# Attention scores with the head dimension's high and low parts stacked in one 128-row matmul, and all head-1 copies on DVE

## The reference

```
z = jnp.einsum("bqhd,bkhd->bhqk", qb, kb).astype(jnp.float32) * scale
strict = s_pos < t_pos
log_keep = jnp.where(strict, jax.nn.log_sigmoid(-z), 0.0)
after = lax.cumsum(log_keep, axis=3, reverse=True) - log_keep
weights = jnp.where(strict, jnp.exp(jax.nn.log_sigmoid(z) + after), 0.0)
outs.append(jnp.einsum("bhqk,bkhd->bqhd", weights.astype(v.dtype), vb))
```

## Time and profile before

| | us |
|---|---|
| median of 3 runs | 2955.57 (2955.53 to 2959.38) |
| the profiled execution | 2955.53 |
| its span, first to last instruction | 2953.8 |
| PE busy in the span | 2770.1 (94%) |
| DVE busy | 1511.2 (51%) |
| ACT busy | 1077.0 (36%) |
| POOL busy | 985.1 (33%) |
| attention stage, within the span | about 1573 to 2525 |

### The profile page before, as it was taken

The page is one execution under the profiler, slowest core; times in us unless marked ns, Lnnn a source line. Parts: engine busy times, 40 slices in busy tenths (PEclk is TensorE's granted clock), DMA queues, the critical chain, the costliest instruction groups (busy, mean ns, idle before and its releaser), DMA issues. The chain is left out here.

```text
span 2953.8 us, 40091 instructions
## 1 busy us (share of the span) xinstructions
PE 2770.1 (94%) x14914; PEld 2031.1 (69%) x14914; DVE 1511.2 (51%) x1689; ACT 1077.0 (36%) x1590; POOL 985.1 (33%) x694
## 2 busy tenths in 40 slices
PE   4999999999999989979997999999999999689998
PEld 3999999888888857756664555555555555368887
DVE  6112445210000010008996888888889888565554
ACT  4010101111111131101114778777778777432221
POOL 1211121121211200007775655656566556200000
PEclk6999999999999999989997999999999999889999
DMA  3232221323212211114444122121221210342331
GB/s 117 85 116 99 79 71 64 114 107 118 74 64 71 78 58 67 45 45 120 129 128 140 58 58 73 37 87 51 58 87 35 82 30 26 117 137 87 98 99 43
DMA packets 165312, 239.96 MB, mean 81 GB/s; under 512 B 11152, under 2 KB 117904, under 8 KB 157504
## 3 DMA queue, kind: packets, MB, share of 16 engines
q1 hardware_dynamic: 163456, 238.25, 25.2%
q10 hardware_dynamic: 1728, 0.03, 0.0%
HBM read 141.49 MB, written 96.76 MB: 81 GB/s over the span
## 5 line engine op out<-in xcount | busy, mean ns | idle before, releaser
L1399 POOL TENSOR_TENSOR a_w<-a_beta,a_rest 128x1024 f32<-128x1024 f32 (+2 forms) x320 | 560.3, 1751 | 341.3 <-DVE a_rest L1351 311.8
L352 PE MATMUL f_acc<-ut_hi,f_w_hi 128*128 128x512 f32 (+2 forms) x1568 | 582.4, 371 | 14.6 <-POOL f_w_lo L337 14.6
L352 PE MATMUL f_acc<-ut_lo,f_w_hi 128*128 128x512 f32 (+2 forms) x1568 | 584.6, 373 | 0.0
L352 PE MATMUL f_acc<-ut_hi,f_w_lo 128*128 128x512 f32 (+2 forms) x1568 | 583.2, 372 | 0.0
L1351 DVE TENSOR_TENSOR_SCAN a_rest<-a_keep,a_rest,a_ones 128x513 f32<-128x513 f32 x384 | 466.8, 1262 | 11.0 <-ACT a_keep L1321 11.0
L1270 PE MATMUL a_turn<-a_ident,a_w 128*128 128x128 f32 (+1 forms) x2432 | 352.7, 280 | 28.1 <-DVE a_wt L1304 26.0
L1270 PEld LDWEIGHTS a_turn<-a_ident,a_w 128*128 128x128 f32 (+1 forms) x2432 | 257.4, 140 | 123.1 <-issue 64.9
L334 POOL TENSOR_TENSOR f_w_hi<-f_stage,f_zero 128x1024 fp32r<-128x1024 f32 x44 | 83.3, 1893 | 770.7 <-DMA f_stage<-in_w_blocks 770.7
L1285 PE MATMUL a_o<-a_wt,a_v 128*64 128x512 f32 (+3 forms) x1408 | 338.5, 559 | 0.0
L352 PEld LDWEIGHTS f_acc<-ut_hi,f_w_hi 128*128 128x128 f32 x1568 | 295.1, 188 | 51.0 <-issue 15.3
L352 PEld LDWEIGHTS f_acc<-ut_lo,f_w_hi 128*128 128x128 f32 x1568 | 295.0, 188 | 34.7
(11 more groups left out here) (172 smaller groups left out, 3415.8 us busy)
## 6 DMA issues: line engine op xcount, KB each, us to landing
f_stage<-in_w_blocks SPq DMA_DIRECT2D x44, 512.0 KB, 5.5
scratch_gate<-f_row_a SPq DMA_DIRECT2D x16, 1024.0 KB, 4.6
o_g<-scratch_mixed SPq DMA_DIRECT2D x32, 512.0 KB, 5.4
scratch_xbc<-f_row_a SPq DMA_DIRECT2D x12, 1032.0 KB, 4.8
s_xc<-scratch_xbc SPq DMA_DIRECT2D x16, 768.0 KB, 5.3
scratch_k_hi<-f_row_a SPq DMA_DIRECT2D x8, 1032.0 KB, 3.9
scratch_k_lo<-f_row_b SPq DMA_DIRECT2D x8, 1032.0 KB, 6.9
n_xin<-in_x SPq DMA_DIRECT2D x16, 512.0 KB, 3.5
```

The source lines that it names most:

```text
L352: last = nc.tensor.matmul(acc[c][:, 0:tn], w[s][:, k, :], u[:, k, t0:t0 + tn], start=(k == 0 and u is ut_hi and w is w_hi), stop=(k == KB ...
L1399: nc.gpsimd.tensor_tensor(w[r % AS][:, :, 0:tn], beta[r % KEEPS][:, :, 0:tn], rest[r % RS][:, :, 1:tn + 1], ALU.mult).then_inc(w_ready, 1)
```

## The change

Three things are edited, all in the attention stage.

The scores are formed in 128-row matmuls, one head at a time. q_high and q_low of a head lie one over the other, in partitions 0 to 63 and 64 to 127 of a new tile `q`, the two heads beside each other. k_high and k_low are each held twice, in the upper and the lower 64 partitions, again with the heads beside each other. One matmul with k_high gives q_high k_high + q_low k_high, one with k_low gives q_high k_low + q_low k_low, a product that was left out before. That is four matmuls a unit in place of six; in diagonal units a head's mask product follows its two.

The transfers follow the layout: each part of each key tensor is loaded by two transfers of 64 partitions, each reading the whole of what one transfer read before. The queries are read once, as before.

`on_act` is now head 0 alone, so that the second head's copy of every fourth block (11 in a head pair) goes from ACT to DVE.

```diff
--- before.py
+++ after.py
@@ -1115,7 +1115,7 @@
     PADS = [pads(n) for n in range(N + 1)]
 
     def on_act(m, h):
-        return h == 0 or m % 4 == 0
+        return h == 0
 
     EVACS = {engine: [sum((on_act(x // 2, x % 2)) == (engine == "act") for x in range(y)) for y in range(2 * N + 1)]
              for engine in ("act", "dve")}
@@ -1131,9 +1131,9 @@
         def ring(name, n, shape, dt=F32):
             return [m_.sbuf(f"a_{name}{r}", list(shape), dt) for r in range(n)]
 
-        k_high, k_low = ring("k_high", 2, (P, T), F32R), ring("k_low", 2, (P, T), F32R)
+        k_high, k_low = ring("k_high", 2, (P, 2, T), F32R), ring("k_low", 2, (P, 2, T), F32R)
         v = ring("v", 2, (P, NT + 1, P))
-        q_high, q_low = ring("q_high", 2, (P, W), F32R), ring("q_low", 2, (P, W), F32R)
+        q = ring("q", 2, (P, 2, W), F32R)
         gate, out = ring("gate", 2, (P, W)), ring("out", 2, (P, W))
         keep, beta = ring("keep", KEEPS, (P, 2, SIDE)), ring("beta", KEEPS, (P, 2, SIDE))
         rest = ring("rest", RS, (P, 2, SIDE + 1))
@@ -1173,8 +1173,10 @@
                 slot = pair % 2
                 t0, t1 = ((0, W + META), (W + META, T))[part]
                 for tile, name in ((k_high, "k_hi"), (k_low, "k_lo")):
-                    sp.dma_start(tile[slot][:, t0:t1].bitcast(F32),
-                                 scratch[name][pair, :, t0:t1]).then_inc(k_loaded[slot][part], 16)
+                    for half in range(2):
+                        sp.dma_start(tile[slot][half * HEAD:(half + 1) * HEAD, :, t0:t1].bitcast(F32),
+                                     scratch[name][pair, :, t0:t1].rearrange("(h p) t -> p h t", h=2)
+                                     ).then_inc(k_loaded[slot][part], 16)
 
             def load_values(pair):
                 slot = pair % 2
@@ -1185,9 +1187,10 @@
 
             def load_queries(ch):
                 pair, c, r = ch // NW, ch % NW, ch % 2
-                for tile, name in ((q_high, "q_hi"), (q_low, "q_lo")):
-                    sp.dma_start(tile[r][:, :].bitcast(F32),
-                                 scratch[name][pair, :, c * W:(c + 1) * W]).then_inc(q_loaded[r], 16)
+                for half, name in enumerate(("q_hi", "q_lo")):
+                    sp.dma_start(q[r][half * HEAD:(half + 1) * HEAD, :, :].bitcast(F32),
+                                 scratch[name][pair, :, c * W:(c + 1) * W]
+                                 .rearrange("(h p) t -> p h t", h=2)).then_inc(q_loaded[r], 16)
 
             def load_gate(ch):
                 pair, c, r = ch // NW, ch % NW, ch % 2
@@ -1231,20 +1234,17 @@
                 if n == 0 or chunk_of(n - 1) != ch:
                     pe.wait_ge(q_loaded[ch % 2], START + 32 * (ch // 2 + 1))
                     if c < 2:
-                        pe.wait_ge(k_loaded[slot][c], START + 32 * (pair // 2 + 1))
+                        pe.wait_ge(k_loaded[slot][c], START + 64 * (pair // 2 + 1))
                 if n >= 2:
                     pe.wait_ge(beta_ready, START + n - 1)
                 t0 = W * (k + 1) if qi is None else W * k
                 tn = width(n)
-                products = ((q_high, k_high), (q_low, k_high), (q_high, k_low))
-                for i, (q_part, k_part) in enumerate(products):
-                    for h in range(2):
-                        rows = slice(h * HEAD, (h + 1) * HEAD)
-                        mm = nc.tensor.matmul(z[n % 2][:, h, 0:tn], q_part[ch % 2][rows, qb * P:(qb + 1) * P],
-                                              k_part[slot][rows, t0:t0 + tn], start=(i == 0),
-                                              stop=(i == len(products) - 1), skip_group_check=True)
-                if diagonal(n):
-                    for h in range(2):
+                for h in range(2):
+                    for k_part in (k_high, k_low):
+                        mm = nc.tensor.matmul(z[n % 2][:, h, 0:tn], q[ch % 2][:, h, qb * P:(qb + 1) * P],
+                                              k_part[slot][:, h, t0:t0 + tn], start=(k_part is k_high),
+                                              stop=(k_part is k_low), skip_group_check=True)
+                    if diagonal(n):
                         if qi is None:
                             z_part, never_part = z[n % 2][:, h, 0:META], never[:, P - META:P]
                         else:
```

## The result

| kernel | median us | runs | span of the profiled execution |
|---|---|---|---|
| before | 2957.08 (2955.53 to 2959.38) | 4 | 2953.8 |
| after | 3011.78 (3010.36 to 3014.28) | 4 | 3009.1 |

The change makes the kernel slower: ratio 1.0185, 95% interval 1.0168 to 1.0203. That is +54.7 us where +17.5 was forecast, and above the range. The two profiled spans differ by 55.3.

The account below looks back on a forecast made before the run. It took DVE to bound three stretches of each head pair and PE the rest. Copies +1.70 and PE -0.23 gave +1.47 per pair, x 8 = +11.8; key loads +5.8; 2955.5 + 11.8 + 5.8 = 2973.1 us, range 2957 to 2990.

Parts of the forecast that it names:

- The copies, +1.70 per pair: On DVE in attention: 11 head-1 copies a pair moved from ACT cost +1.70 us per pair, bounds 0 and +3.4.
- the three runs: Stretches of a head pair, in chunks 1, 2 and 3, where DVE never stops; copies add +0.17, +0.59 and +0.94.
- The switch regained: On PE: changing from 64 to 128 rows costs about 0.10 ahead of the turns and 0.05 in them, regained by the edit.
- The rival in which neither comes back: On PE: neither switch nor short passes regained, about +2.2 us per pair more, +18 us, 2991; chance 0.10.
- 4 x 0.228 + 0.054 for one load: PE's new scores in a full off-diagonal unit: four passes and one weight load, 0.97 us where it was 0.91.
- the units that I had named as PE's: Units where PE sets the pace: second of chunk 0 to last diagonal of chunk 1, last three diagonals of chunks 2, 3.
- -0.23: PE's whole term per head pair, from the diagonal units where PE sets the pace: a gain of 0.23 us.
- My upper bound, +0.5 to +1.1: PE's term per pair if a narrow 128-row pass can't go under the 0.11 us of a pair of loads.
- Off the diagonal +0.01 to +0.03: PE's extra time in each full off-diagonal unit, in us; +0.17 if the switch were not regained, mostly hidden either way.
- Ahead of it stand 2.11 MB more: +5.8: Start of attention: doubled key loads delay chunk 1's first unit by 5.8 us at 364 GB/s.
- My bound of +10: Upper bound in us on the keys' loads at the start, if 64-partition transfers are slower and the clock rises later.
- Later pairs ... free, for the queue's next transfers too: Key loads of later pairs cost nothing: issued a pair (120 us) ahead, with DMA busy a fifth of the stage.

Follow-up runs that it names:

- the run with the masks last: The changed kernel with both mask products behind both heads' scores in diagonal units, as the kernel before has them: 3005.91 us, ratio 1.0165.
- keys' transfers halved: The kernel before with every key transfer split into two of 64 partitions, bytes and layout unchanged: 2961.27 us, ratio 1.0014.

## Why the prediction was wrong

- **Direction and place: right.** Slower, in the pairs and at the start, nowhere else.
- **The copies, +1.70 per pair: right.** Alone they cost +1.67. The count from start to start, the three runs and the gaps held, run by run (0.19, 0.59 and 0.93 for 0.17, 0.59 and 0.94), so this isn't luck; DVE's waits for ACT above 0.5 are gone.
- **The switch regained: right.** From the last pass to the turns 0.24, the turns 0.96 (forecast 0.97 behind full-height work). The rival in which neither comes back is refuted by the first of these.
- **"4 x 0.228 + 0.054 for one load": wrong, the first failed step.** I halved the 0.108 of two loads. They had run side by side, so one load shows the same 0.11. The Trainium skill, "TensorEngine Tiling (Array Packing)", Key Properties, has the rule that I passed over, in the same short list as the one that I cited: different tiles can load weights and multiply in parallel. The load rows agree (0.19 for two half-height loads, 0.19 for one full one). In the changed kernel a unit's first pass is 0.34, and no narrow pass falls below 0.11. From scores to turns the diagonal units take, as medians over the stage, before and after: 144 columns 0.61 and 0.66, 272: 0.70 and 0.81, 400: 0.87 and 1.03, 16: 0.50 and 0.55, 512: 1.01 and 1.23. That is +0.59 in a group of five where I had -0.20. Over the units that I had named as PE's (nine, and the last three of two chunks) it sums to 0.54 + 0.59 + 2 x 0.43 = +2.0 per pair; the runs show +2.14. The forecast had -0.23, an error of 2.4 per pair, 19 us in all. My upper bound, +0.5 to +1.1, held the minimum of a pass but not the load behind each mask product, which the run with the masks last prices at 0.79 per pair.
- **Off the diagonal +0.01 to +0.03:** it is +0.07 (2.94 to 3.01), from the same load. It stayed mostly hidden, as forecast for sizes under +0.17.
- **"Ahead of it stand 2.11 MB more: +5.8": wrong, the second failed step,** as large an error as the first: +24.6. I priced bytes at the 364 GB/s of transfers that write 128 partitions, and the change writes 64 at a time. Of this, some 22 are the half-partition rate with all that follows from it: the run with the same bytes in 128 partitions has about 3 left. My bound of +10 named slower 64-partition transfers, but no row of before had one and I gave them no factor. The Trainium skill, "SBUF — State Buffer", The DMA port swizzle, states that partitions 0 to 63 reach one half of the ports and 64 to 127 the other. By that rule each half transfer has half the ports, and 237 against 461 ns agrees.
- **"Later pairs ... free, for the queue's next transfers too":** true from pair 1 on, but not for pair 1's own loads, which are issued ahead of chunk 2's queries. By the run that moves them, this backlog is about 10 of the 24.6. The two sizes are not to be added: the backlog is itself a child of the low rate.
- **The copies and the scores overlap:** 1.67 + 2.48 = 4.15 alone, 3.81 together. The forecast let them add up; a small error.
- **Slips in the working, too small to matter:** the doubled keys are 2.11 MB more per pair, not 2.06 (the sum used 2.11), and by the forecast's own rule 144 columns come to 0.43 after the change, not 0.45.

**Left open.** With half of head 1's copies on ACT an undisturbed pair takes 117.9, between 119.78 and the 114.7 of all on ACT but far from midway. Three waits of PE for DVE are left in it, and no run shows why these three stay. Nor is it shown why the clock fell behind two of them and not behind the others. It also wasn't tried whether a better order of the first loads would bring more than the 2 us of moving the values.

## What to carry to other kernels

Price a weight load by what runs beside it: two half-height loads in one step cost as much as one full one, so fewer instructions can be more time. Price a transfer by how many partitions it writes and how it spreads over the DMA engines before its bytes, and follow what stands behind it in its queue. When a wait names the engine that is late, see whether its work fits elsewhere: here taking from DVE the 33 head-1 copies that it makes in a pair gave 1.4%, and giving it the other 11 cost 0.5%. And before two executions are compared at one point, see how far apart they already were where the programs are still the same.

## What the runs showed of the hardware

- Two 64-row weight loads of 128 columns at the same time last 0.19 us together (before), one 128-row load 0.19 too (after). In a stream of narrow fp32r passes of 16 to 144 columns the starts are no closer than 0.11, and so are those of the loads (masks behind both heads).
- Two bf16 loads of 128 columns last 0.12 together, and the two passes behind them take 0.12 (masks behind both heads).
- An fp32r pass whose load stands behind a bf16 product takes 0.31 for 512 columns, where it is 0.23 behind its own kind (after).
- 6144-byte packets: 237 ns into 128 partitions (before), 427 (keys' transfers halved) and 461 ns (after) into 64, and the rate falls with them from 364 to 245 and 227 GB/s.
- A transfer whose source repeats outermost twice moves 53 GB/s; with the repeat inside it moves with the rest at 362.
- PE idle for 6.42 us came back at a granted clock of 0.50, the lower of its two levels (after). With half of head 1's copies on ACT the clock read 0.52 for 3.4 us behind waits of 1.00 and 1.24, and stayed up behind another of 0.99.
- The same program ahead of the attention ended at times 4.0 us apart over thirteen profiled executions.
